# Output projection of a decoder step joined to the last attention head: partial products over seven heads, sample rows first

## The chip, the cores and the metric

One core of a Trainium2 chip runs one program that computes the whole step. Its engines are TensorE (PE, with its weight loads PEld), VectorE (DVE), ScalarE (ACT), GpSimd (POOL) and SyncE (SP), which here issues DMAs. Each runs its own list of instructions in order and meets the others only at semaphores. The metric is the device time of the program in microseconds; lower is better.

## The reference

One layer of a decoder trunk for 1024 prompt rows and 8 sample rows, all of width 1024 in float32:

```python
h = x * (1 + sc1) + sh1
q, k, v, u, gates = split(h @ w_in)                  # 8 heads, q1/q2/k1/k2 of 64, v of 128
o = attend(rope(q), rope(k), v, lam)                 # softmax(q1 k1) - lam * softmax(q2 k2)
attn_out = head_rmsnorm(o, subln_g) * (1 - lam_init)
merged = sigmoid(g_pool) * pool_mixer(u) + sigmoid(g_attn) * attn_out
x = layer_norm(alpha * x + (1 + g1) * (merged @ w_out), ln1_g, ln1_b)
h2 = x * (1 + sc2) + sh2
x = layer_norm(alpha * x + (1 + g2) * hier_moe(h2), ln2_g, ln2_b)   # 16 experts, 2 per row
```

The change concerns `merged @ w_out` and what lies on either side of it: the last head in front, the layer norm, `h2` and the routing of rows to experts behind.

## The kernel before

The program has five stages with a barrier on all five engines between them (`stage_end`: each adds one to a semaphore and waits for all). Stage 0 computes the modulation and `h`; stage 1 the pooling branch and the attention heads; stage 2 the output projection, layer norm, `h2`, router logits and routing; stage 3 the experts in 32 slots of 128 rows; stage 4 combines and normalises. Float32 products are made of three reduced-precision ones: each operand is split in a high part (ScalarE's copy) and a remainder (a subtraction on VectorE or GpSimd), and `mm3` (lines 856 to 860) runs high times remainder, remainder times high, high times high into one PSUM sum.

**Stage 1.** It begins with the sample state: SP loads it (line 632), TensorE transposes it (940 to 943) and waits until VectorE has copied it (1853) before the first projection piece. Then come twelve pieces of `u` with the pooling products. A piece is 24 matmuls of 344 columns (`piece`, 927 to 936). The heads loop (1120 to 1188) has eight steps for each head, one for each block of 128 rows. In a step TensorE makes the scores, ScalarE the exponentials (`exps`), VectorE maxima and the combination of the two softmaxes. `turn` transposes blocks of weights, `weights` on ScalarE and VectorE splits them, `product` multiplies them with v. There are ten turns for each head; four of them (6 to 9) run inside the next head, and for the last head behind the loop (1189 to 1191). Between these, TensorE runs pieces of the next head's input projection, as `filler`, to fill its waits; which ones is written in `step_pieces` (541 to 546). The last head has only its own six gate pieces left, in steps 4 to 7. A head ends with `squares` and `inverse_rms` (the RMS norm) and VectorE's `merge` (1983 to 1991), which adds the two branches; SP stores the merged rows of a head in DRAM (`merged_stored`, 684 to 686). The split `h` (`hT`) and the splits of `w_in` fill the SBUF tensor `R` up to the heads' own operands.

**Stage 2.** The split w_out takes the place of `hT`. SP loads w_out in eight parts of 512 KB and, from DRAM, each tile's merged columns for all eight heads (`tile3`, 733 to 740). ScalarE and VectorE split w_out, ScalarE and GpSimd (`m_rest`, 2335) the columns. `project` (1197 to 1209) makes 48 matmuls of 512 columns for one tile of 128 rows; nine tiles, the last with the 8 sample rows. Two pairs of PSUM banks take turns, and two buffers of columns. VectorE's `norm3` (2078 to 2088) does gate, residual and layer norm; GpSimd's `second_input` (2340 to 2347) makes `h2`; TensorE transposes it (`turn_rows3`), ScalarE copies it (`columns`), TensorE makes the logits (`router`), VectorE adds the bias (`logits`). For the sample tile the tables of the prompt are overwritten by those of the samples (771 to 773, 2103 to 2106). Then routing runs on VectorE (2125 to 2191) until the barrier.

## Time and profile before

| quantity | value |
|---|---|
| median of three runs | 1553.48 us (1551.81 to 1553.80) |
| profiled execution, its time | 1553.97 us |
| span of its instructions | 1552.1 us |
| TensorE busy, share of the span | 1315.6 us, 85% |
| VectorE busy | 988.1 us, 64% |
| ScalarE busy | 716.6 us, 46% |
| GpSimd busy | 284.5 us, 18% |
| TensorE on the chain that ended last | 67% |

All positions in the text are microseconds from the start of the span. A busy time is that of an engine's instructions; matmuls overlap a little, so the time that one costs is read from the distance of starts, not from its own duration. Idle time stands in brackets behind an instruction, with what ended it. The granted clock is TensorE's: 1.00 is 2.4 GHz, 0.50 is 1.2 GHz.

### The profile page before, as it was taken

The page shows a single profiled execution, that of the slowest core. Times are in us where ns is not written, and L with a number is a line of the kernel's source. Part 1 is how long each engine was busy: PE and PEld are TensorE (multiplying, and loading weights), DVE is VectorE, ACT ScalarE, POOL GpSimd, SP SyncE. Part 2 cuts the span into 40 slices and gives each one's busy share as a digit, 9 for nine tenths or more (in the row PEclk, how much of TensorE's full clock was granted, in tenths as well). Part 3 has the DMA queues.
Part 4 walks back from the last instruction along what each step waited for, and adds up shares of the span by engine and source line. Part 5 has one row for each costly group of instructions (what it writes and reads, how often), then busy time and mean ns, then how long its engine had stood idle before and what let it go on. Part 6 is the DMA issues. An engine that isn't in the chain of part 4 may idle for free.

```text
span 1552.1 us, 24627 instructions
## 1 busy us (share of the span) xinstructions
PE 1315.6 (85%) x8748; PEld 1139.0 (73%) x8748; DVE 988.1 (64%) x1484; ACT 716.6 (46%) x1249; POOL 284.5 (18%) x161
## 2 busy tenths in 40 slices
PE   6698989999999999999998783899549999999800
PEld 3488979898988989899897572677338887888600
DVE  2334357576674758657485633456459998999669
ACT  1344334444543535444454424011118897999612
POOL 1422111011111111111111001344231111111050
PEclk9899989999999999999999785899659999999955
DMA  9686433232233323233232106633139989556393
GB/s 313 199 267 207 128 87 91 80 90 77 83 96 87 105 71 94 75 84 102 85 97 65 49 7 222 189 109 123 45 106 328 319 298 370 184 202 222 124 294 141
DMA packets 211362, 229.53 MB, mean 148 GB/s; under 512 B 18070, under 2 KB 185178, under 8 KB 211131
## 3 DMA queue, kind: packets, MB, share of 16 engines
q1 hardware_dynamic: 196011, 173.52, 35.3%
q0 software_dynamic: 6976, 25.23, 5.0%
q10 hardware_dynamic: 8280, 29.51, 4.8%
q8 instruction: 59, 0.97, 0.3%
q14 instruction: 36, 0.29, 0.1%
HBM read 173.20 MB, written 46.79 MB: 142 GB/s over the span
## 4 chain that ended last, share of the span: by engine, by line
PE 67%; DVE 14%; ACT 5%; DMA 5%; issue 4%; SPq 3%; POOL 2%; ACTq 0%; DVEq 0%; POOLq 0%
PE S L858 6%; PE S L860 6%; PE S L859 6%; PE T L931 4%; PE T L932 4%; PE PB L931 4%; PE T L935 4%; PE PB L935 4%; PE PB L932 4%; PE S L1021 3%; ACT F L1345 3%; DVE F L1931 2%; PE T L1047 2%; PE T L1107 2%; DVE sm L1915 2%
## 5 line engine op out<-in xcount | busy, mean ns | idle before, releaser
L1345 ACT ACTIVATE R<-F 128x1024 fp32r<-128x1024 f32 (+3 forms) x302 | 292.6, 1014 | 125.0 <-DVE F L1806 46.0
L858 PE MATMUL S<-R 128*128 128x512 f32 (+1 forms) x528 | 213.2, 404 | 34.6 <-ACT R L1345 19.6
L859 PE MATMUL S<-R 128*128 128x512 f32 (+1 forms) x528 | 209.4, 397 | 0.0
L860 PE MATMUL S<-R 128*128 128x512 f32 (+1 forms) x528 | 209.3, 396 | 0.0
L2316 POOL TENSOR_TENSOR R<-F,R 128x1024 fp32r<-128x1024 f32 x40 | 99.7, 2494 | 593.5 <-ACT R L1345 593.5
L931 PE MATMUL T<-R 128*128 128x344 f32 x480 | 158.6, 335 | 0.0
L931 PE MATMUL PB<-R 128*128 128x344 f32 x480 | 157.6, 333 | 0.0
L932 PE MATMUL T<-R 128*128 128x344 f32 x480 | 153.0, 323 | 0.0
L932 PE MATMUL PB<-R 128*128 128x344 f32 x480 | 152.0, 321 | 0.0
L858 PEld LDWEIGHTS S<-R 128*128 128x128 f32 (+1 forms) x528 | 99.9, 189 | 61.4 <-issue 35.7
L1345 ACT ACTIVATE R<-T 128x512 fp32r<-128x512 f32 x144 | 82.7, 596 | 118.2 <-PE T L1047 76.0
L1345 ACT ACTIVATE F<-T 128x344 f32<-128x344 f32 (+5 forms) x100 | 42.1, 425 | 205.7 <-PE T L935 113.8
L1345 ACT ACTIVATE F<-S,sm 128x256 f32<-128x256 f32 (+7 forms) x128 | 93.6, 739 | 79.5 <-DVE sm L1915 42.4
L860 PEld LDWEIGHTS S<-R 128*128 128x128 f32 (+1 forms) x528 | 99.6, 189 | 23.4
L859 PEld LDWEIGHTS S<-R 128*128 128x128 f32 (+1 forms) x528 | 99.9, 189 | 21.3
L931 PEld LDWEIGHTS T<-R 128*128 128x128 f32 x480 | 91.5, 191 | 1.9 <-issue 1.8
L1912 DVE TENSOR_REDUCE sm<-S 128x1 f32<-128x128 f32 (+3 forms) x32 | 15.7, 491 | 120.3 <-PE S L1024 120.3
L2381 POOL DMA_INDIRECT F<-h_d,idxs x32 | 46.4, 1448 | 250.4 <-PE T L1267 230.6
L932 PEld LDWEIGHTS T<-R 128*128 128x128 f32 x480 | 91.7, 191 | 0.7 <-issue 0.7
L931 PEld LDWEIGHTS PB<-R 128*128 128x128 f32 x480 | 90.8, 189 | 1.7 <-issue 1.6
L932 PEld LDWEIGHTS PB<-R 128*128 128x128 f32 x480 | 90.9, 189 | 1.0 <-issue 1.0
L2199 DVE TENSOR_TENSOR R<-F,R 128x1024 fp32r<-128x1024 f32 x62 | 75.8, 1222 | 20.6 <-ACT R L1345 20.6
(258 smaller groups left out, 2747.5 us busy)
## 6 DMA issues: line engine op xcount, KB each, us to landing
F<-in_w_ada SPq DMA_DIRECT2D x24, 1024.0 KB
F<-in_w_in SPq DMA_DIRECT2D x44, 512.0 KB, 4.0
F<-in_w_e_gate SPq DMA_DIRECT2D x16, 1024.0 KB
F<-in_w_e_up SPq DMA_DIRECT2D x16, 1024.0 KB
F<-in_w_e_down SPq DMA_DIRECT2D x16, 1024.0 KB
y_d<-F ACTq DMA_DIRECT2D x32, 512.0 KB, 7.4
out<-F SPq DMA_DIRECT2D x24, 512.0 KB, 4.0
F<-F SPq DMA_DIRECT2D x192, 43.0 KB, 1.9
```

What stands on the lines that cost most here:

```text
L858: mm(out, w[0], m[1], start=start, stop=False)
L859: mm(out, w[1], m[0], start=False, stop=False)
L860: return mm(out, w[0], m[0], start=False, stop=stop)
L931: mm(bank[:, 0:PIECE], whl[b][0][:, k, :], x[1][:, k, :], start=(k == 0), stop=False)
L932: mm(bank[:, 0:PIECE], whl[b][0][:, k, :], x[0][:, k, :], start=False, stop=False)
L935: last = mm(bank[:, 0:PIECE], whl[b][1][:, k, :], x[0][:, k, :], start=False, stop=(k == KC - 1))
L1021: mm(S[:, m * SEQ + a:m * SEQ + a + n], qhl[x][half, i * P:(i + 1) * P], khl[y][half, a:a + n], start=(x == 0 and y == 1), stop=(x == 0 an ...
L1047: last = tr(TB[0][:, (2 * j + t) * P:(2 * j + t + 1) * P], block_rows(h, 2 * p + t)[:, (2 * g + j) * P:(2 * g + j + 1) * P], ident)
L1345: return nc.scalar.activation(out, in_, func, **kw)
L2199: TT(gu[b][1][:, k, 0:FF], raw_g[b][:, k, :], gu[b][0][:, k, 0:FF].bitcast(F32), ALU.subtract).then_inc(g_lo, 1)
L2316: nc.gpsimd.tensor_tensor(whl[c % 2][1], wraw2[c % 2], whl[c % 2][0].bitcast(F32), ALU.subtract).then_inc(w_lo.sem, 1)
L2381: nc.gpsimd.indirect_dma_start(out=xg[b], out_offset=None, in_=h2_d, in_offset=bass.IndirectOffsetOnAxis(ap=idxs[:, tile:tile + 1], axis=0 ...
```

## The change

- The barrier between heads and output projection is gone; four stages are left. Every engine goes on in its own list, with semaphores for each buffer.
- In the last head the six gate pieces run one in each of the steps 0 to 5. Their results go to the places of the head's q and k rows.
- When these pieces are done, `hT` is free, and the split w_out goes there. Its eight parts are loaded from step 1 of the last head on, into five buffers in place of the four in one block. ScalarE splits them in steps 5 to 7 and in the last turns, GpSimd makes all eight remainders.
- TensorE makes the products of the first three tiles over heads 0 to 6 inside the last head and behind it (`unit`), the product over head 7 after the merge, with columns split straight from SBUF (`last_hi`, `last_lo`). The sample rows are tile 0.
- Three PSUM pairs and three buffers of columns take turns, where there were two; the PSUM tensors are laid out anew. The first three tiles take heads 0 to 6 from DRAM, the other six all eight heads after the last store.
- Transposes and router products stand at written places between quarters of a tile, transposes in two halves through one bank; the loops are unrolled. All logits stay in one PSUM bank, and the bias is added once at the end.
- The layer norm's scale and shift goes from VectorE to ScalarE (`normal`); the additions of 1 to the first gate are part of VectorE's first instruction. VectorE makes `h2` of the last tile itself. The samples' tables have buffers of their own and come with the others; VectorE's last merge waits for all thirteen tables.
- In stage 1 the transposes of the sample state come behind the second piece, not ahead of the first.

The core of the diff:

```diff
-    TB = [ctx.enter_context(nc.psum_tensor(f"T{i}", [P, 512], F32)) for i in range(2)]
+    T0 = ctx.enter_context(nc.psum_tensor("T0", [P, 512], F32))
+    AB = ctx.enter_context(nc.psum_tensor("AB", [P, 1024], F32))
     OB = ctx.enter_context(nc.psum_tensor("OB", [P, 512], F32))
-    PB = ctx.enter_context(nc.psum_tensor("PB", [P, 512], F32))
+    TB = [T0, AB[:, 0:512]]
+    PB = AB[:, 512:1024]
...
-            return [first + j for j in {4: (0,), 5: (1,), 6: (2, 3), 7: (4, 5)}.get(i, ())]
+            return [first + i] if i < 6 else []
...
+            def w_out_chunk(k):
+                b = k % 5
+                if k >= 5:
+                    sp.wait_ge(wo_lo, k - 4)
+                    sp.wait_ge(wo_hi, k - 4)
+                sp.dma_start(wo32[b], wov[:, k, :]).then_inc(wo_landed[b].sem, 16)
+
+            def columns3(n):
+
+                b, (t, rows) = n % 3, at3(n)
+                heads = 7 if n < 3 else 8
+                if n >= 3:
+                    sp.wait_ge(mg_st, 16 * H)
+                    sp.wait_ge(m_hi, n - 2)
+                    sp.wait_ge(m_lo, n - 2)
+                sp.dma_start(mt32[b][:, 0:heads, 0:rows], mg_d.rearrange("k p n -> p k n")[:, 0:heads, t * P:t * P + rows]).then_inc(m_landed[b].sem, 16)
+
+            def rows3(n):
+
+                t, rows = at3(n)
+                if n >= 2:
+                    sp.wait_ge(var_done, n - 1)
+                sp.dma_start(x3[n % 2][0:rows, :], x_p[t * P:t * P + rows, :] if n else x_s).then_inc(x3_landed[n % 2], 16)
...
+            def first_w_out():
+                chunk_split(sp, N_CHUNKS - 2)
+                chunk_split(sp, N_CHUNKS - 1)
+                for k in range(3):
+                    w_out_chunk(k)
...
+                sp.wait_ge(kout_st, 16 * H)
+                w_out_chunk(3)
+                sp.wait_ge(vout_st, 16 * H)
+                v_lo.wait(sp, H - 1, 0)
+                w_out_chunk(4)
...
+            def last_tables():
+                for k in range(5, 8):
+                    w_out_chunk(k)
+                gate0_used.wait(sp, H - 1, 2)
+                table(l1b, I["ln1_b"].to_broadcast([P, D]))
+                os_ready.wait(sp, H - 1, 0)
+                table(g1s[0:NS, :], mod_d[1:9, 2 * D:3 * D])
+                table(sc2s[0:NS, :], mod_d[1:9, 4 * D:5 * D])
+                comb.wait(sp, H - 1, 7)
+                columns3(2)
+                rows3(0)
+                for k, dst, src in ((5, l1g, I["ln1_g"]), (6, sc2b, mod_d[0:1, 4 * D:5 * D]), (7, sh2b, mod_d[0:1, 3 * D:4 * D])):
+                    sp.wait_ge(wo_hi, k + 1)
+                    sp.wait_ge(wo_lo, k + 1)
+                    table(dst, src.to_broadcast([P, D]))
+                table(sh2s[0:NS, :], mod_d[1:9, 3 * D:4 * D])
+                t_ready.wait(sp, H - 1, 9)
+                rows3(1)
+
...
             merged_stored(H - 1)
+            columns3(3)
+            columns3(4)
+            columns3(5)
+            rows3(2)
+            columns3(6)
+            rows3(3)
+            columns3(7)
+            rows3(4)
+            columns3(8)
+            sp.wait_ge(h2_done, 1)
...
-        pe.wait_ge(ld_pool, 16)
-        for g in range(4):
-            last = tr(TB[0][:, 120 * g:120 * g + 120], stt[0:120, g * P:(g + 1) * P], ident[0:120, 0:120])
-        last.then_inc(stT_ready, 1)
-        pe.wait_ge(stT_copied, 1)
...
+                if n == 1:
+                    state_columns()
...
+        def unit(n, k, halves=(0, 1)):
+
+            rows = at3(n)[1]
+            if k == 0:
+                pe.wait_ge(m_hi, n + 1)
+                pe.wait_ge(m_lo, n + 1)
+                if n == 0:
+                    copied(pe, LAST + 4)
+                    copied(pe, LAST + 5)
+                else:
+                    exp_done.wait(pe, H - 1, 7)
+                if n == 2 and 0 in halves:
+                    ln_done.wait(pe, H - 1, 0)
+            if k == KC - 1:
+                mb_hi.wait(pe, n + 1)
+                mb_lo.wait(pe, n + 1)
+            if n == 0:
+                pe.wait_ge(wo_hi, k + 1)
+                pe.wait_ge(wo_lo, k + 1)
+            for q in halves:
+                last = mm3(WB[n][0:rows, 512 * q:512 * q + 512], [m[:, k, 0:rows] for m in mhl[n]],
+                           [w[:, k, 512 * q:512 * q + 512] for w in wo], start=(k == 0), stop=(k == KC - 1))
+            if k == KC - 1:
+                last.then_inc(wout_ready, 1)
...
+                if h == H - 1 and i >= 6:
+                    todo = [lambda k=k: unit(0, k) for k in ((0, 1), (2, 3))[i - 6]]
...
+            unit(*((0, 4), (0, 5), (0, 6), (1, 0))[n - 6])
             product(H - 1, n)
-        exp_done.wait(pe, H - 1, 7)
+        for k in range(1, 4):
+            unit(1, k)
         squares(H - 1)
-        stage_end(pe, 1)
-
-
-        def project(n, b, rows, first=False):
-            pe.wait_ge(m_hi, n + 1)
-            pe.wait_ge(m_lo, n + 1)
-            if not (isinstance(n, int) and n < 2):
-                pe.wait_ge(wout_used, n - 1)
-            for q in range(2):
-                for k in range(KC):
-                    if first and q == 0:
-                        pe.wait_ge(wo_hi, k + 1)
...
+        def project(n, q, ks):
+            b = n % 3
+            if q == 0 and ks[0] == 0:
+                pe.wait_ge(m_hi, n + 1)
+                pe.wait_ge(m_lo, n + 1)
+                pe.wait_ge(wout_used, n - 2)
+            for k in ks:
+                last = mm3(WB[b][:, 512 * q:512 * q + 512], [m[:, k, :] for m in mhl[b]],
+                           [w[:, k, 512 * q:512 * q + 512] for w in wo], start=(k == 0), stop=(k == KC - 1))
+            if q == 1 and ks[-1] == KC - 1:
+                last.then_inc(wout_ready, 1)
...
+        BETWEEN = {4: ((), (lambda: ta(0),), (), (lambda: tb(0),)),
+                   5: ((lambda: router(0), lambda: ta(1)), (lambda: tb(1),), (lambda: router(1),), ()),
+                   6: ((lambda: ta(2),), (lambda: tb(2),), (lambda: router(2), lambda: ta(3)), (lambda: tb(3),)),
+                   7: ((lambda: router(3), lambda: ta(4)), (lambda: tb(4),), (lambda: router(4),), (lambda: ta(5),)),
+                   8: ((lambda: tb(5),), (lambda: router(5), lambda: ta(6)), (lambda: tb(6),), (lambda: router(6),))}
+        for n in range(3, 9):
+            for e in range(4):
+                project(n, e // 2, range(4 * (e % 2), 4 * (e % 2) + 4))
+                for extra in BETWEEN.get(n, ((),) * 4)[e]:
...
+        def w_out_hi(k):
+            wo_landed[k % 5].wait(act, 16 * (k // 5 + 1))
+            if k == 0:
+                ready(act, LAST + 5)
+            act_(wo[0][:, k, :], wo32[k % 5]).then_inc(wo_hi, 1)
...
+                    if h == H - 1:
+                        w_out_hi(0)
+                        merged_hi(0)
...
+            if n < 9:
+                w_out_hi(n - 1)
         outputs(H - 1, 3)
         squares(H - 1)
+        merged_hi(2)
         inverse_rms(H - 1)
-        stage_end(act, 1)
...
+        def normal(n):
+            rows = at3(n)[1]
+            off3_done.wait(act, n + 1)
+            act_(y3[0:rows, :], y3[0:rows, :], ACT.Identity, scale=rstd1[0:rows, :], bias=off3[0:rows, :]).then_inc(norm3_done.sem, 1)
...
+            if h == H - 1:
+                tables3()
...
+        def last_lo(n):
+
+            t, rows = at3(n)
+            mb_hi.wait(dve, n + 1)
+            TT(mhl[n][1][:, 7, 0:rows], poolc[:, t * P:t * P + rows], mhl[n][0][:, 7, 0:rows].bitcast(F32), ALU.subtract).then_inc(mb_lo.sem, 1)
...
+        def sums3(n):
+
+            b, rows = n % 2, at3(n)[1]
+            y = y3[0:rows, :]
+            dve.wait_ge(wout_ready, n + 1)
+            mark(STT(out=y, in0=(g1b if n else g1s)[0:rows, :], scalar=1.0, in1=WB[n % 3][0:rows, :], op0=ALU.add, op1=ALU.mult), wout_used, n + 1)
+            dve.wait_ge(x3_landed[b], X3 + 16 * (n // 2 + 1))
+            V(STT(out=y, in0=x3[b][0:rows, :], scalar=ALPHA, in1=y, op0=ALU.mult, op1=ALU.add))
             for q in range(2):
-                V(nc.vector.bn_stats(stat[0:rows, q, :], y[0:rows, 512 * q:512 * q + 512]))
...
+        def last_input():
+
+            dve.wait_ge(h2_st[0], 16 * 4)
+            dve.wait_ge(h2T_ready, 14)
+            V(TT(h2t[0], x1t[0], sc2b, ALU.mult))
+            TT(h2t[0], h2t[0], sh2b, ALU.add).then_inc(h2_last.sem, 1)
+
+        for n in range(9):
+            sums3(n)
+            offset3(n)
+            affine3(n)
+        last_input()
...
+        def w_out_lo(k):
+            wo_landed[k % 5].wait(pool, 16 * (k // 5 + 1))
+            pool.wait_ge(wo_hi, k + 1)
+            nc.gpsimd.tensor_tensor(wo[1][:, k, :], wo32[k % 5], wo[0][:, k, :].bitcast(F32), ALU.subtract).then_inc(wo_lo, 1)
...
+        w_out_lo(0)
+        m_rest(0)
+        w_out_lo(1)
+        w_out_lo(2)
+        m_rest(1)
+        for k in range(3, KC):
+            w_out_lo(k)
+        m_rest(2)
+        m_rest(3)
+        m_rest(4)
+        pool.wait_ge(tab_landed, 16 * TABLES)
+        pool.wait_ge(tab_ready, 1)
+        pool.wait_ge(mg_st, 16 * H)
+        for n in range(8):
+            second_input(n)
+            if n < 4:
+                m_rest(n + 5)
+        pool.wait_ge(h2T_ready, 18)
```

## Rows read from the trace of the kernel before

**Rows 1.** Busy time by stretch: PE, PEld, DVE, ACT, POOL, clock, DMA, GB/s.
```profile
180.00:930.00 750.00, 709.10 (x4813) 645.11 (x4813) 471.97 (x800) 328.74 (x671) 92.36 (x37) 0.97 0.28 81
930.00:1151.00 221.00, 145.68 (x686) 116.10 (x684) 115.68 (x179) 44.03 (x61) 72.91 (x32) 0.77 0.36 121
```
**Rows 2.** Chain that ended last, projection stage: start, duration, what.
```profile
933.84 1.62 issue
...
938.09 1.16 PE T L1083 x2
...
944.89 2.65 DMA mg_d<-F
...
997.03 0.43 PE S L858
...
1051.65 1.69 PE PB L1223 x16
...
1065.47 1.70 PE PB L1223 x16
...
1105.71 3.57 PE PB L1223 x16
```
**Rows 3.** Timeline of TensorE: start, duration, instruction, idle time before and what ended it.
```profile
958.82 0.76 PE L858 MATMUL S<-R 128*128 128x512 f32 x1 [19.59 <-ACT R L1345]
...
995.41 0.77 PE L858 MATMUL S<-R 128*128 128x512 f32 x1 [7.42 <-POOL R L2337]
```
**Rows 4.** Timeline of VectorE, last full tile and routing.
```profile
1079.47 1.22 DVE L2081 TENSOR_TENSOR F<-S,F 128x1024 f32<-128x1024 f32 x1 [3.91 <-PE S L860]
...
1086.51 1.22 DVE L2088 TENSOR_TENSOR F<-F 128x1024 f32<-128x1024 f32 x1
...
1118.45 0.19 DVE L1791 TENSOR_REDUCE F<-F 128x9 f32<-128x36 f32 x1
...
1150.42 0.17 DVE L2191 TENSOR_SCALAR te<-F 1x32 int32<-1x32 f32 x1
```
**Rows 5.** Timeline of TensorE, two matmuls of the projection, 41 apart.
```profile
978.31 0.39 PE L858 MATMUL S<-R 128*128 128x512 f32 x1
...
987.61 0.39 PE L860 MATMUL S<-R 128*128 128x512 f32 x1
```
**Rows 6.** Chain that ended last, start of the pooling stage.
```profile
67.41 2.92 DMA F<-in_state_pool
...
72.33 0.65 PE S L931
```
**Rows 7.** Timeline of TensorE in head 7, with the waits before.
```profile
860.79 2.63 PE L1083 MATMUL S<-F,cst 128*128 128x344 f32 x4 [3.62 <-DVE R L1935]
...
871.62 2.18 PE L1021 MATMUL S<-R 64*128 64x512 f32 x12 [4.49 <-ACT F L1345]
...
905.11 0.41 PE L931 MATMUL PB<-R 128*128 128x344 f32 x1
...
908.98 0.28 PE L858 MATMUL OB<-R 128*128 128x256 f32 x1
...
920.58 0.45 PE L858 MATMUL OB<-R 128*128 128x256 f32 x1 [1.50 <-DVE R L1935]
```
**Rows 8.** Timeline of ScalarE: a split of w_out, a normalisation of the last stage.
```profile
951.51 1.06 ACT L1345 ACTIVATE R<-F 128x1024 fp32r<-128x1024 f32 x1 [9.31 <-DMA F<-in_w_out]
...
1502.28 1.24 ACT L1345 ACTIVATE F<-F 128x1024 f32<-128x1024 f32 x1
```
**Rows 9.** GpSimd and VectorE side by side, and VectorE's line in the stage (min/median/max, ns).
```profile
992.82 2.33 POOL L2337 TENSOR_TENSOR R<-F,R 128x1024 fp32r<-128x1024 f32 x1
...
993.11 2.60 DVE L2075 TENSOR_SCALAR F<-F,sm 128x1024 f32<-128x1024 f32 x1
...
L2075 DVE TENSOR_SCALAR F<-F,sm x9: 801/814/2597, 983.8 to 1102.1; 128x1024 f32<-128x1024 f32 x8, 8x1024 f32<-8x1024 f32 x1
```
**Rows 10.** Loads of merged columns by SP (line 737), issue to landing.
```profile
DMA to landing us min/median/max: 5.5/7.0/9.8
```

More of the change, by code:

```diff
@@ new lines, in turn_rows3 @@
+        def turn_rows3(n, c, bank):
+            rows = at3(n)[1]
+            if c == 0:
+                if n < 8:
+                    pe.wait_ge(h2_done, n + 1)
+                else:
+                    h2_last.wait(pe, 1)
+            if bank is T0:
+                pe.wait_ge(h2T_copied, 2 * n + c)
+            for k in range(4 * c, 4 * c + 4):
+                last = tr(bank[:, (k % 4) * P:(k % 4) * P + rows], h2t[n % 2][0:rows, k * P:(k + 1) * P], ident[0:rows, 0:rows])
+            last.then_inc(h2T_ready, 1)
@@ L1427, in take @@
             if n == 12 and h:
-                merged.wait(act, h - 1, 0)
+                if h < H - 1:
+                    merged.wait(act, h - 1, 0)
+                else:
+                    kt_ready.wait(act, h, 4)
             ready(act, g)
@@ new lines, in _ @@
+        ca, cb = (lambda n: columns(n, 0, T0)), (lambda n: columns(n, 1, T0))
+        tile3(3)
+        tile3(4)
+        deviation(0)
+        normal(0)
+        deviation(1)
+        x1_store(0)
+        normal(1)
+        tile3(5)
+        deviation(2)
+        x1_store(1)
+        normal(2)
+        h2_store(0)
+        ca(0)
+        x1_store(2)
+        h2_store(1)
+        tile3(6)
+        cb(0)
+        deviation(3)
+        normal(3)
+        ca(1)
+        cb(1)
+        x1_store(3)
@@ new lines, in _ @@
+        h2_store(2)
+        tile3(7)
+        deviation(4)
+        normal(4)
+        ca(2)
+        x1_store(4)
+        cb(2)
+        h2_store(3)
+        tile3(8)
+        deviation(5)
+        normal(5)
+        ca(3)
+        x1_store(5)
+        cb(3)
+        h2_store(4)
+        ca(4)
+        deviation(6)
+        normal(6)
+        cb(4)
+        x1_store(6)
+        h2_store(5)
+        ca(5)
+        cb(5)
+        deviation(7)
+        normal(7)
+        ca(6)
+        x1_store(7)
@@ L1681, in _ @@
+        h2_store(6)
+        cb(6)
+        ca(7)
+        h2_store(7)
+        cb(7)
+        deviation(8)
+        normal(8)
+        h2_store(8)
+        columns(8, 0, T0)
+        columns(8, 1, Sb[0])
+        x1_store(8)
         act.wait_ge(route_exp, 1)
@@ L2336, in m_rest, with second_input @@
             pool.wait_ge(m_hi, n + 1)
-            nc.gpsimd.tensor_tensor(mhl[b][1][:, :, 0:rows], mt32[b][:, :, 0:rows], mhl[b][0][:, :, 0:rows].bitcast(F32), ALU.subtract)\
+            nc.gpsimd.tensor_tensor(mhl[b][1][:, 0:heads, 0:rows], mt32[b][:, 0:heads, 0:rows], mhl[b][0][:, 0:heads, 0:rows].bitcast(F32), ALU.subtract)\
                 .then_inc(m_lo, 1)
-        def second_input(n, b, rows, before):
+        def second_input(n):
+            b, rows = n % 2, at3(n)[1]
+            scale, shift = (sc2b, sh2b) if n else (sc2s, sh2s)
@@ L2352, in _ @@
[L2352 to L2364 removed]
+            if n >= 2:
+                pool.wait_ge(h2_st[b], 16 * (n // 2))
+                pool.wait_ge(h2T_ready, 2 * n - 2)
```

417 lines of the change are left out of this document (186 added, 231 removed).

## Prediction

> **What bounds the kernel now.** I read the views in this order: the page's slices, busy time by stage, the waits and the timeline of TensorE around the end of the heads, the chain, and last the timelines of VectorE, ScalarE and GpSimd in the same place. In the heads TensorE is the bound: 709 of 750 us busy at a mean granted clock of 0.97 [rows 1]. In the 221 us from the end of the heads to the start of the experts it is busy for 146 us at a mean clock of 0.77 [rows 1]. So this stage has 75 us in which TensorE does nothing, and it is here that a reordering can pay. The stretch has three holes. First: the last product of head 7 ends at 933.84, six sums of squares run from 935.46 to 939.25 [rows 2], and the next matmul, the first of the output projection, starts at 958.82 after 19.6 us of idle time [rows 3]. The chain through that hole is the merge (done at 944.87), the store of the merged rows (2.65 us, lands 947.5) [rows 2], barrier, load of w_out, split. Second: the third tile waits 7.4 us for GpSimd [rows 3], whose remainder for it was queued behind the first tile's h2. Third: the eight sample rows come last and cost as much on every engine as a full tile. VectorE takes the last full tile at 1079.47, and routing begins at 1118.45, 39 us later [rows 4]. Routing itself runs to 1150.6 and I expect none of its 32.1 us to change.
>
> Between the holes the projection is bound by TensorE. At full clock 41 matmuls of 512 columns lie between 978.31 and 987.61, 0.227 us each; at half clock the chain has 0.43 each [rows 2, 5]. One unit (one contraction block, both halves of the output, three split products each) is six matmuls, 1.36 us. A tile is eight units, 10.9 us. From router to router in the loop it is 1065.47 - 1051.65 = 13.8 us [rows 2], so one router and one set of transposes cost 2.9 us between two tiles.
>
> **Part 1, the state transposes at the start of the pooling stage.** SP issues the state load at 67.41, right behind the barrier; TensorE waits for it, transposes, waits for VectorE's copy and starts its first real product at 72.33 [rows 6]. The change lets the first product start at about 67.4 and puts the four transposes two pieces later. They take at most the time from landing (70.33) to 72.33 less VectorE's copy, about 1.2 us. Gain 4.9 - 1.2 = 3.7 us at most; zero at worst, if the modulation weights, which are loaded in the same stretch and are needed 5 us earlier, are late. I take 3. TensorE bounds the stages behind, so it should last.
>
> **Part 2, inside head 7.** Six gate pieces of 3.87 us (905.11 to 908.98) [rows 7] were run at steps 4 to 7 as 1, 1, 2, 2; now one runs at each of steps 0 to 5. In steps 0 and 1 each falls into a wait for VectorE like that of 1.50 us at 920.58 [rows 7], so each adds some 2.4. In step 2 it lies in the 3.62 us wait, in step 3 in the 4.49 us wait [rows 7], which cost nothing more; and the array stays at full clock, worth about 1.4. Step 4 thus starts 3.5 us late. In steps 6 and 7 four pieces (15.5 us) make room for four units of the sample rows (5.5). Of these 10 us I count only 2.8, because what is late next is not TensorE: VectorE has its maxima and combinations in these steps anyway, and each unit waits for its eighth of w_out, which is ScalarE 1.06 [rows 8] and then GpSimd 2.3 to 2.4 [rows 9] after a ScalarE instruction that itself waits for the exponentials. Those splits are queued on ScalarE ahead of the head's own weights and outputs; the products stand behind the units on TensorE. So the first of the last four turns starts 0.7 late. These turns went round in 3.9 us each: turn, ScalarE, VectorE, then the product after a 1.5 us wait at half clock. A unit fills the wait; but ScalarE 0.6 + 1.06 and GpSimd 2.4 lie between a turn and the second unit behind it, so I get 12.3 us instead of 15.4 with the first wait for a remainder. The last product ends at 933.8 + 0.7 + 0.5 - 3.1 = 931.9. Bounds: 8 us earlier (the 10 us come in full), 8 us later (each of the eight remainders costs a microsecond).
>
> **Part 3, from the last product to the fourth tile.** TensorE has three units (4.1), the squares (3.8 in the trace [rows 2], after a wait; with none I take 2.5, between that and half of it), ten units (13.6) and the three last blocks (4.1): 24.3 us, to 956.2. Meanwhile the merge: squares end at 931.9 + 6.6 = 938.5; before it took from 939.25 to 944.87, 5.6 us, so it ends at 944.1. VectorE now also waits inside the merge for thirteen tables, the last issued behind the last w_out remainder. That is about 931, with a landing of up to 9.8 like the loads of [rows 10]: 941, and the reciprocal roots it waits for anyway come at 941.6. Free, but with under 1 us in hand. The three last-head splits follow in 1.5 us, ahead of 956. So the merge is covered by products. Not covered is the way of the next tile: store 2.65, load median 7.0 (5.5 to 9.8) [rows 2, 10], ScalarE 1.06, GpSimd 2.4, hand-overs 0.6, in all 13.7: ready at 957.8. TensorE waits 1.6 us and then runs some nine matmuls at half clock (0.2 more each, 1.8): it goes on at 959.6. Bounds: no wait (956.2), or 9.8 for the load and a 4 us store (962).
>
> The barrier and the w_out load behind it are gone, and so is the third tile's wait for GpSimd, since its columns are split ahead of any h2. Three pairs let VectorE fall behind by three tiles. It needs 8.3 us a tile (1079.47 to 1087.73) [rows 4] plus 0.8 for the hand-over to ScalarE and up to 1 for GpSimd in the way. It starts at 954 and meets TensorE's 13.8 us rhythm at the sixth tile or so, before any product must wait for its pair.
>
> **Part 4, the loop.** Six tiles, each with a router and transposes: 6 x 13.8 = 82.9, one more set of transposes 0.9, and 1 for places where a copy of transposed columns stands on ScalarE behind a tile that VectorE still has. Last projection done at 1044.4; with part 1 at 1041.4. Before: 1079.5.
>
> **Part 5, the tail.** The last tile is now a full one, the sample rows went first, their tables came early, and the load before 1097 is gone. VectorE: 8.3 for the tile less 0.81 plus ScalarE's normalisation (1.24 for the same form in the last stage [rows 8]) plus 0.4 for a small instruction and hand-overs: 9.1. Then h2 on VectorE, two instructions, 2.5, in place of GpSimd's 4.8. Router 3.57 at half clock [rows 2], the eight transposes 1.8 (in the loop the 2.9 less the router's 1.7 is 1.2; twice 0.9 is the matmuls alone), copy 0.7, logits 0.6. Sum 18.3, where it was 39. Routing starts at 1059.7 instead of 1118.45: 58.7 us earlier, and everything behind keeps its length; the first experts' weights still come before it. The chip's profiled execution of before took 1553.97 (0.5 over the median of the three runs), so the sum is 1553.97 - 58.7 = 1495.3, and 1494.8 against the median: **1495**.
>
> **A rule that speaks against it.** At 993.11 VectorE's scale-and-shift takes 2.60 us, while GpSimd's subtraction started at 992.82 and ends at 995.15; the median of the line is 0.81 [rows 9]. So a GpSimd instruction can hold a VectorE one until it is through. The change gives GpSimd the eight w_out remainders, which VectorE computed before in a stretch with nothing else to do.
> The Trainium skill (SBUF — State Buffer, Who interferes with whom) says that the two share a port pair as an exclusive lock, that VectorE's 2-port modes and its instructions with two SBUF inputs contend with GpSimd's reads, and that the first to start blocks the other fully. By that rule every combination of head 7 may be held; the trace agrees at 993, but the line's median stayed at 0.81 beside a busy GpSimd. What it would do to the time is the second rival below.
>
> **The rivals.**
> 1. *The load takes the barrier's place.* The fourth tile's columns wait for the store, then for one of three loads issued together. For it: landings of up to 9.8 us; against it: 24 us of products stand before. At the bounds above plus a second late tile: 6 us more, 1501.
> 2. *GpSimd becomes the bound of head 7.* Eight remainders, each blocking a VectorE instruction for up to 2.60 - 0.81 = 1.8 us, 14 us in all: 1509. For it: rows 9, and the products queue behind the units. Against it: the median of that line, 0.81, with GpSimd busy in the same stretch.
> 3. *More than I count.* Steps 6 and 7 give TensorE's 10 us in full, no wait at the fourth tile: 10 us less, 1485.
> 4. *The overlap doesn't come about.* Units find no split w_out and hold up the head; the projection's first 21 units (28.6 us) then lie after the products as before: about 1524.
> 5. *Slower than before.* The projection runs at half clock from end to end: 432 matmuls at 0.20 us more are 86 us, 1581. It decides from 59 us lost, that is if over two thirds of the 432 run at half clock. Against it: before, full clock was back at 978.31 after the 19.6 us hole [rows 3, 5], and the changed order has fewer holes.
>
> **How the numbers follow.** Forecast 0.60 (1487 to 1503), rival 1 0.13, rival 2 0.10, rival 3 0.11, rival 4 0.04, rival 5 0.02. The range for 8 in 10 takes the forecast with rivals 1, most of 2 and most of 3: 1483 to 1511. A measurement can tell 0.2% (3 us) from no change. Only rival 5 is slower; faster 0.97, same 0.01, slower 0.02.
>
> **What would show it.** Right: no idle time over 3 us on TensorE between the last turns and the last projection; the last product of head 7 within 8 us of 931 (928 with part 1); the last projection near 1041; 18 us from there to the first routing maximum; 32 us of routing. Part 1: the first product of the pooling stage near 67.4. Wrong: idle time at the fourth tile over 4 us (rival 1); VectorE's combinations in head 7 at 2 us or more, or units waiting for GpSimd (rival 2); a clock of 0.5 inside the loop (rival 5).

## The result, and the profile after

The changed kernel takes 1506.55 us (median of 4 runs, 1503.01 to 1508.82) where the kernel before took 1553.62: a ratio of 0.9697, 95% interval 0.9685 to 0.9709. The forecast was 1495 with a range of 1483 to 1511. So the range held the time, and the point was 11.5 us too low. The profiled execution of the changed kernel took 1508.82 us, with a span of 1506.6.

First the page: TensorE's busy time and granted clock by slices, and the chain by engine. Up to the end of the projection (the first 28 slices) the clock now never falls below 8 tenths; the 5 and the 6 are the tail and the routing.

```profile
PE 1307.6 (87%) x8748; PEld 1132.1 (75%) x8748; DVE 995.8 (66%) x1472; ACT 726.3 (48%) x1261; POOL 308.4 (20%) x167
PEclk9989989999999999999999999999569999999955
PE 68%; DVE 16%; ACT 5%; issue 4%; DMA 4%; SPq 2%; POOL 1%; ACTq 0%; DVEq 0%; POOLq 0%
```

Busy time by stretch (PE, PEld, DVE, ACT, POOL, clock, DMA, GB/s): the end of head 7 with the first units, the projection from there on, and the tail up to the routing.

```profile
930.00:958.00 28.00, 26.97 (x130) 20.89 (x129) 8.89 (x11) 10.33 (x15) 6.83 (x3) 1.00 0.48 145
958.00:1057.00 99.00, 90.10 (x455) 74.03 (x454) 71.31 (x72) 26.83 (x37) 57.22 (x22) 0.95 0.42 145
1057.00:1075.00 18.00, 12.03 (x65) 10.95 (x63) 9.47 (x12) 5.21 (x7) 0.00 (x0) 0.61 0.22 87
```

The hole of 19.6 us in [rows 3] is gone: TensorE is busy for 27 of 28 us there. In the loop it is busy for 90 of 99 us; of those 9 us the forecast had 1.6, at the fourth tile, and 1 for late copies. TensorE's timeline with its waits: the start of the pooling stage (three rows), head 7 (two), the fourth tile, and one of the loop.

```profile
62.50 1.08 PE L965 MATMUL S<-F 128*9 128x64 f32 x64 [1.25 <-DMA F<-in_b_ada]
...
69.77 0.66 PE L982 MATMUL S<-R 128*128 128x344 f32 x1 [3.75 <-DVEq L249]
...
78.94 1.90 PE L965 MATMUL S<-F 128*9 128x64 f32 x64 [3.05 <-DMA F<-in_b_ada]
...
900.25 0.48 PE L909 MATMUL AB<-R 128*8 128x512 f32 x1 [2.88 <-POOL R L2545]
...
907.49 0.59 PE L909 MATMUL AB<-R 128*8 128x512 f32 x1 [2.99 <-POOL R L2539]
...
963.06 0.47 PE L909 MATMUL AB<-R 128*128 128x512 f32 x1 [2.24 <-POOL R L2545]
...
999.74 1.12 PE L1315 MATMUL T<-cst,F 128*128 128x128 f32 x4 [2.48 <-ACT F L1443]
```

VectorE in the projection. The first tile, the offset of 8x1 elements (L2283) and two instructions of 1024 columns are long; then come the last two tiles, which wait for TensorE again, and the first maximum of the routing.

```profile
958.14 1.21 DVE L2271 SCALAR_TENSOR_TENSOR F<-F,AB 8x1024 f32<-8x1024 f32 x1 [8.49 <-PE AB L911]
...
963.07 2.10 DVE L2283 SCALAR_TENSOR_TENSOR sm<-sm 8x1 f32<-8x1 f32 x1 [0.23 <-DVE sm L2282]
...
970.24 2.35 DVE L2273 SCALAR_TENSOR_TENSOR F<-F 128x1024 f32<-128x1024 f32 x1
...
982.27 2.28 DVE L2273 SCALAR_TENSOR_TENSOR F<-F 128x1024 f32<-128x1024 f32 x1
...
1042.64 1.22 DVE L2271 SCALAR_TENSOR_TENSOR F<-F,S 128x1024 f32<-128x1024 f32 x1 [5.98 <-PE S L911]
...
1057.16 1.22 DVE L2271 SCALAR_TENSOR_TENSOR F<-F,S 128x1024 f32<-128x1024 f32 x1 [5.75 <-PE S L911]
...
1075.36 0.19 DVE L1982 TENSOR_REDUCE F<-F 128x9 f32<-128x36 f32 x1
```

GpSimd and ScalarE beside them. The first row is GpSimd's remainders of the fourth and fifth tile's columns, one behind the other until 965.16. GpSimd's second instruction of h2 takes 3.23 us beside a busy VectorE, and ScalarE's split of the fourth tile's columns waits for TensorE, not for the load.

```profile
959.40 5.76 POOL L2545 TENSOR_TENSOR R<-F,R 128x1024 fp32r<-128x1024 f32 x2 [17.23 <-ACT R L1443]
...
969.12 2.39 POOL L2556 TENSOR_TENSOR F<-F 8x1024 f32<-8x1024 f32 x1 [3.96 <-DVE F L2294]
...
983.55 3.23 POOL L2557 TENSOR_TENSOR F<-F 128x1024 f32<-128x1024 f32 x1
...
958.20 1.06 ACT L1443 ACTIVATE R<-F 128x1024 fp32r<-128x1024 f32 x1 [8.88 <-PE AB L911]
```

The row at 970.24 can be read off against GpSimd's. VectorE's instruction starts 1.1 us after GpSimd's at 969.12, which ends at 971.51; 1.08 us after that, VectorE's is done (1.22 is its usual length). The offset at 963.07 is the same: 0.16 us of work, through (965.17) only when GpSimd's remainder is.

### The profile page after: what moved, and what is told of

Its sections match the earlier page's. It is cut to its first block, busy times and chain, and to the rows that moved or that the text cites. A ratio compares the mean times of both kernels' runs of the same rounds, so it can differ in the third digit from the quotient of the medians.

```text
span 1506.6 us, 24502 instructions
## 1 busy us (share of the span) xinstructions
PE 1307.6 (87%) x8748; PEld 1132.1 (75%) x8748; DVE 995.8 (66%) x1472; ACT 726.3 (48%) x1261; POOL 308.4 (20%) x167
## 4 chain that ended last, share of the span: by engine, by line
PE 68%; DVE 16%; ACT 5%; issue 4%; DMA 4%; SPq 2%; POOL 1%; ACTq 0%; DVEq 0%; POOLq 0%
PE AB L982 8%; PE AB L983 8%; PE AB L986 8%; PE S L909 6%; PE S L911 6%; PE S L910 6%; ACT F L1443 4%; PE S L1078 3%; DVE sm L2106 2%; DVE F L2122 2%; PE T L1166 2%; PE T L1104 2%; PE OB L909 1%; PE S L924 1%; ACT R L1443 1%
## 5 line engine op out<-in xcount | busy, mean ns | idle before, releaser
L1443 ACT ACTIVATE R<-F 128x1024 fp32r<-128x1024 f32 (+4 forms) x305 | 292.7, 1006 | 100.1 <-DVE F L1997 48.0
L982 PE MATMUL AB<-R 128*128 128x344 f32 x960 | 315.7, 333 | 0.0
L983 PE MATMUL AB<-R 128*128 128x344 f32 x960 | 304.6, 321 | 0.0
L909 PE MATMUL S<-R 128*128 128x512 f32 x480 | 193.9, 404 | 1.8 <-ACT F L1443 1.6
L911 PE MATMUL S<-R 128*128 128x512 f32 x480 | 189.1, 394 | 0.0
L910 PE MATMUL S<-R 128*128 128x512 f32 x480 | 188.9, 394 | 0.0
L982 PEld LDWEIGHTS AB<-R 128*128 128x128 f32 x960 | 181.7, 189 | 3.4 <-issue 3.2
L983 PEld LDWEIGHTS AB<-R 128*128 128x128 f32 x960 | 182.0, 190 | 1.7 <-issue 1.7
L986 PE MATMUL AB<-R 128*128 128x344 f32 x960 | 171.6, 320 | 0.0
L1443 ACT ACTIVATE F<-AB 128x344 f32<-128x344 f32 (+1 forms) x126 | 56.1, 447 | 221.7 <-PE AB L986 221.0
L986 PEld LDWEIGHTS AB<-R 128*128 128x128 f32 x960 | 155.7, 188 | 0.0
L1443 ACT ACTIVATE R<-T 128x512 fp32r<-128x512 f32 x112 | 66.9, 597 | 113.2 <-PE T L1104 71.3
L909 PEld LDWEIGHTS S<-R 128*128 128x128 f32 x480 | 91.6, 191 | 21.2 <-issue 2.9
L911 PEld LDWEIGHTS S<-R 128*128 128x128 f32 x480 | 91.3, 190 | 20.1
L910 PEld LDWEIGHTS S<-R 128*128 128x128 f32 x480 | 91.4, 191 | 17.9
L2593 POOL DMA_INDIRECT F<-h_d,idxs x32 | 50.4, 1576 | 244.2 <-PE AB L1365 227.2
L2126 DVE TENSOR_TENSOR R<-T,R 128x512 fp32r<-128x512 f32 x80 | 54.7, 684 | 45.0 <-ACT R L1443 45.0
L1443 ACT ACTIVATE F<-S 9x64 f32<-9x64 f32 (+3 forms) x159 | 53.6, 349 | 50.8 <-PE S L986 29.6
```

The lines of the kernel that those rows point to most:

```text
L909: mm(out, w[0], m[1], start=start, stop=False)
L910: mm(out, w[1], m[0], start=False, stop=False)
L911: return mm(out, w[0], m[0], start=False, stop=stop)
L982: mm(bank[:, 0:PIECE], whl[b][0][:, k, :], x[1][:, k, :], start=(k == 0), stop=False)
L983: mm(bank[:, 0:PIECE], whl[b][0][:, k, :], x[0][:, k, :], start=False, stop=False)
L986: last = mm(bank[:, 0:PIECE], whl[b][1][:, k, :], x[0][:, k, :], start=False, stop=(k == KC - 1))
```

## The experiments

Positions in a profile shift by some us with the early stages. So each kernel is read by four marks: Z, the second modulation piece of stage 0 (62.50 above); X, head 6's scores at 797.40 in the changed kernel (793.78 in the one before); E, the end of head 7's last product; L, VectorE's first instruction of the last tile. T is the first product of the fourth tile.

| kernel | Z to X | X to E | E to T | T to L | median us | ratio to before |
|---|---|---|---|---|---|---|
| before | 733.7 | 140.1 | | | 1553.5 | 1 |
| changed | 734.9 | 139.7 | 26.0 | 94.1 | 1506.6 | 0.9697 |
| c1 changed again | 735.0 | 140.0 | 26.0 | 94.1 | 1505.8 | 0.9685 [0.9661, 0.9710] |
| e1 state first | 733.2 | 138.3 | 25.9 | 92.1 | 1504.7 | 0.9689 [0.9673, 0.9705] |
| e2 tile 0 early | 733.4 | 139.8 | 23.6 | 92.7 | 1501.6 | 0.9675 [0.9651, 0.9699] |
| e3 rows in PSUM | 734.1 | 139.9 | 30.9 | 83.9 | 1502.4 | 0.9671 [0.9652, 0.9691] |
| e4 units behind | 732.7 | 140.7 | 38.4 | 94.2 | 1517.8 | 0.9765 [0.9750, 0.9780] |
| e6 e2 with e3 | 733.6 | 138.3 | E to L 111.6 | | 1497.4 | 0.9639 [0.9626, 0.9653] |
| e7 h2 halved | 733.7 | 138.2 | 25.9 | 90.7 | 1502.8 | one run |
| e8 e1, e2, e3 | 733.2 | 138.4 | E to L 111.6 | | 1496.0 | 0.9626 [0.9613, 0.9639] |
| e9 thin remainders | 733.9 | 133.3 | 25.9 | 94.0 | 1499.0 | one run |
| e10 e8, ScalarE's order | 733.0 | 139.8 | E to L 107.8 | | 1494.3 | 0.9618 [0.9604, 0.9631] |

From L to the routing's first maximum it is 18.2 to 18.4 us in each of them, and from there to the end of the span 430.4 to 434.1. The intervals of e1, e2 and e3 overlap that of c1, so for these three the marks carry the argument and not the time; e4, e6, e8 and e10 lie clear of it.

**c1, the changed kernel again.**

> The changed kernel itself, as the control for the three beside it on the same chip. Expected 1503 to 1509 us, as measured so far; the place of the last projection's end, of the first routing maximum and of the first scores of head 7 are read from it.

1505.84 us, and every mark behind Z within 0.3 us of the first profile. The kernel repeats; what moves is Z (2.7 us earlier here).

**e1, the state's transposes back where they were** (part 1 undone).

```diff
+        state_columns()
+        pe.wait_ge(stT_copied, 1)
...
-                if n == 1:
-                    state_columns()
```

> The changed kernel with the transposes of the sample state back ahead of the first piece, as before. My theory: the earlier start is eaten by the modulation weights that come late (TensorE waited 3.05 us for them at 78.94 and then ran a piece at half clock), so this kernel is 0 to 2 us faster than the control. The prediction's own term: it is 3 us slower than the control.

The first product of the pooling stage starts late again, as in [rows 6]:

```profile
72.38 0.66 PE L982 MATMUL S<-R 128*128 128x344 f32 x1 [0.82 <-DVE F L2043]
```

but the wait for the modulation weights behind the first pieces (3.05 us at 78.94 above) shrinks to 0.54, and Z to X is 1.7 us shorter than in the changed kernel. Over all profiles, Z to X is 732.7 to 735.0 with the transposes moved (mean 733.9 of eight) and 733.0 to 733.7 with them first (mean 733.3 of four). 1504.67 against 1505.84 is no difference that these runs can tell. The move gains nothing: the pieces start 4.9 us earlier (67.53 in c1) and wait for the modulation's weights.

**e2, tile 0's last block early:** the last head's unit of the sample rows runs before the second half of tile 2, not behind all ten units.

```diff
+        unit(0, 7)
         for k in range(7):
             unit(2, k, (0,))
-        for n in range(3):
+        for n in range(1, 3):
```

> The changed kernel with one unit moved: the last block of tile 0 (the sample rows) runs between the two halves of tile 2, not behind them. Theory A (the wait at the fourth tile is for tile 0's column buffer, and VectorE's queue of tiles bounds what follows): VectorE starts tile 0 about 5 us earlier, the 2.2 us wait of TensorE at the fourth tile shrinks to under 1, and the kernel is 2 to 5 us faster than the control. Rival B (the store and load of the merged columns bound the fourth tile, and TensorE bounds the rest): the wait stays and the time stays within 1 us.

The 2.24 us at the fourth tile are gone, since tile 0's column buffer comes free before the next split needs it:

```profile
957.54 0.39 PE L909 MATMUL AB<-R 128*128 128x512 f32 x1
...
959.21 0.15 DVE L2283 RECIPROCAL sm<-sm 8x1 f32<-8x1 f32 x1 [4.83 <-ACT sm L1444]
```

E to L falls by 3.9 us (120.1 to 116.2). VectorE starts tile 0 4.8 us earlier behind E, but then waits 4.83 us for ScalarE's root: the root is queued behind two splits, and the second of them waits for TensorE. So theory A holds by the marks and rival B does not; the time, 1501.6 against 1505.8, is not resolved.

**e3, the rows being normalised stay in their PSUM pair.** Three of VectorE's instructions of 1024 columns in each tile then read one operand from PSUM and one from SBUF instead of two from SBUF (the first one read the pair before, and the statistics have one input); GpSimd's work is the same. ScalarE's normalisation works in the pair too. The pair comes free with x1 instead of with the first instruction.

```diff
-            y = y3[0:rows, :]
+            y = WB[n % 3][0:rows, :]
...
+            dve.sem_inc(wout_used, 1)
```

> The changed kernel with the layer norm's row kept in its PSUM pair through all steps, so that no large VectorE instruction of the norm has two inputs in SBUF; the same instructions otherwise, and each pair is held until the tile is done. Theory A (GpSimd holds VectorE's instructions, 2.3 us of each tile's 11.5, and that backlog costs 9 us by the last projection): no large instruction of the norm over 1.4 us, a tile in 9.5 us or less, last projection 5 to 9 us earlier, time 1498 to 1502. Rival B (the place of the transposes and copies in the lists bounds, not VectorE's speed): tiles in 9.5 us, but the last projection within 1.5 us of the control. Rival C (a pair held longer makes TensorE wait for it): 3 us or more slower than the control.

VectorE's timeline in e3, and GpSimd's beside it, then the fourth tile:

```profile
974.47 1.23 DVE L2273 SCALAR_TENSOR_TENSOR S<-F,S 128x1024 f32<-128x1024 f32 x1
...
974.03 2.41 POOL L2558 TENSOR_TENSOR F<-F 128x1024 f32<-128x1024 f32 x1
...
1012.26 2.10 DVE L2283 SCALAR_TENSOR_TENSOR sm<-sm 128x1 f32<-128x1 f32 x1
...
964.37 0.77 PE L909 MATMUL AB<-R 128*128 128x512 f32 x1 [7.16 <-DVEq L2296]
```

Started 0.44 us behind GpSimd's, the same line that took 2.35 us now takes its 1.23, and GpSimd's takes 2.41. No instruction of 1024 columns in the loop is over 1.23 us; only the offset, whose operands all lie in SBUF, is still held. T to L is 83.9 us, 10.2 less than in the changed kernel. TensorE is busy through all of it, and nine of its matmuls run at half clock. The gain is half eaten at the fourth tile, which waits 7.16 us for tile 0's pair: E to L falls by 5.3 us only. T thus comes 4.9 us later, which lets VectorE catch up, so e3 alone leaves open how much of the 10.2 is that; e10 below, with T at 23.6 us behind E, needs 84.3 for the same stretch. Theory A holds for the instructions, but not for every tile: most take 8.9 to 9.8 us, two take 12.9 and 13.3, with waits of 2.8 and 2.9 us for ScalarE's root. Rival B does not hold. Rival C's wait for a pair is there, at one place, but the kernel is not slower.

**e4, no units inside head 7:** the eight of steps 6 and 7 and of the four turns run behind its last product.

```diff
-                if h == H - 1 and i >= 6:
-                    todo = [lambda k=k: unit(0, k) for k in ((0, 1), (2, 3))[i - 6]]
...
-            unit(*((0, 4), (0, 5), (0, 6), (1, 0))[n - 6])
```

> The changed kernel with the eight units of steps 6 and 7 and of the four turns of head 7 taken out of the head and put behind its last product; all else as changed. This prices the filling alone. Theory (the units fill waits of TensorE, at the price of 3 us waits for GpSimd's remainders at two of them): the last product of head 7 comes 3 to 6 us earlier than in the changed kernel, eight units more (10.9 us) then stand behind it, and the loop that follows is as before, so the last tile's sums come 3 to 8 us later and the time is 1509 to 1514. Rival (the units in the head gain nothing, since each wait for a remainder costs what it fills): last product 10 to 11 us earlier, the same time as the changed kernel, 1506.

```profile
903.02 0.58 PE L909 MATMUL OB<-R 128*128 128x256 f32 x1 [5.20 <-DVE R L2125]
...
932.03 0.58 PE L909 MATMUL OB<-R 128*128 128x256 f32 x1 [1.41 <-DVE R L2125]
```

Both theories miss. The last product comes 0.7 us later than with the units, not 3 to 11 earlier, and E to T grows by 12.4. The whole is 12.0 us slower. So the eight units in the head cost nothing at all: without them TensorE waits for VectorE instead, and no matmul there waits for GpSimd.

**e9, thin remainders.** What is left out: GpSimd takes 64 of 1024 columns of each remainder of w_out.

> The changed kernel, but GpSimd takes only the first 64 of 1024 columns of each of the eight remainders of w_out (the other columns of the remainder keep what the memory held, so the rows behind are other numbers; only the marks up to the routing are read). It takes away about 18 us of GpSimd's work in and before head 7. Theory (GpSimd's remainders hold VectorE there and TensorE waits for both): VectorE's two combinations of 3.1 and 3.3 us take 1.15 and 1.28 as before the change, the combination with the gate 0.5 instead of 2.1, TensorE's waits for GpSimd in head 7 (3.2, 2.7, 1.0, 1.0, 0.5, 0.4) go to under 1 in all, the last product of head 7 ends 5 to 8 us nearer to the first scores of head 6 (140.0 in the changed kernel) and everything behind follows. Rival (the head is paced by ScalarE's and VectorE's own chain, and the held instructions lie beside it): the instructions shorten but the last product comes at most 2 us earlier.

GpSimd's first long one in head 7 and VectorE's combination, first in the changed kernel (904.85 and 905.17), then the combination of e9:

```profile
904.85 5.67 POOL L2539 TENSOR_TENSOR R<-F,R 128x1024 fp32r<-128x1024 f32 x2 [4.70 <-ACT R L1443]
...
905.17 3.12 DVE L2122 SCALAR_TENSOR_TENSOR F<-F,sm 128x896 f32<-128x896 f32 x1
```

```profile
901.13 1.15 DVE L2122 SCALAR_TENSOR_TENSOR F<-F,sm 128x896 f32<-128x896 f32 x1
...
912.89 1.28 DVE L2122 SCALAR_TENSOR_TENSOR F<-F,sm 128x1024 f32<-128x1024 f32 x1
```

X to E falls by 6.7 us, and the time of the one run by as much (1498.97). Against the shorter of head 7's two lengths (last section) it is 5.0. One part of the theory misses: the first unit still waits 2.79 us for GpSimd, for a remainder of merged columns that itself waits for ScalarE. Head 7 is thus paced by the chain of ScalarE, VectorE and GpSimd; GpSimd's eight remainders cost it 5.0 to 6.7 us, and the units themselves nothing. In e4 the combinations are held as before (3.13 and 3.29 us) and the head stays long though TensorE waits for no remainder. That speaks for VectorE's holds as the way the price is paid; but TensorE's granted clock at the end of the head is also lower in e4 (0.70 from 892.8 to 933.6, against 0.91 in c1 from 894.8 to 934.9), and no run separates the two.

**e7, GpSimd's multiplication left out.** h2 is then x1 plus the shift.

> The changed kernel, but GpSimd leaves out the multiplication of h2 by its scale for tiles 0 to 7 (h2 is then x1 plus the shift; the experts' inputs and the routing are other numbers, so only the marks up to the routing are read). Theory (an instruction of GpSimd with both inputs in SBUF and one of VectorE exclude each other): half as many of VectorE's instructions in the loop are held at 2 us or more (13 in the changed kernel's seven first tiles), none of the held ones where GpSimd is idle, VectorE's period falls from 11.8 to 10.5 us or less, and the last tile's sums come 4 to 9 us nearer to the last product of head 7 (120.1 us in the changed kernel). Rival (VectorE's long instructions come from something else, PSUM or the DMA traffic): as many long ones, and 120 us.

Nine of VectorE's instructions in the loop are over 2 us, where c1 has eleven (the expectation's 13 was a miscount). E to L is 116.6, 3.5 less: below the bound given, and the count is not halved; a tile takes VectorE 11.0 us (11.5 in c1), not 10.5. Leaving out half of h2 takes away fewer meetings than e3 makes harmless, since the remainders and the other half of h2 still meet VectorE. By itself e7 would not carry the cause; e3 does.

**e6, e2 and e3 together,** with tile 0's row left in SBUF so that its pair comes free at once, and **e8,** the same with e1.

> Tile 0's last block runs early (as in e2), and the rows being normalised stay in their PSUM pair for tiles 1 to 8 (as in e3), while tile 0's row still leaves its pair with the first VectorE instruction. In e3 no product of the loop waited any more, but the fourth tile waited 7.2 us for tile 0's pair, because the pair was held until x1 was through. Theory (GpSimd holds VectorE's instructions that have both inputs in SBUF; the pair of tile 0 costs e3 its gain): no VectorE instruction of 1024 columns over 1.4 us, no wait at the fourth tile, from its first product to the last tile's sums 84 to 85 us (94.1 in the changed kernel, 83.9 in e3), from the last product of head 7 to there 107 to 109 us (120.1 in the changed kernel); 11 to 12 us less than the changed kernel, about 1494. Rival (the two gains of e2 and e3 are of the same wait and don't add): 1500. Rival (ScalarE's order bounds the loop): VectorE waits for ScalarE's root in more tiles than e3's three, and 1498 or more.

> As e6, and the state's transposes stand before the first product of the pooling stage again (part 1 undone, as in e1). Theory (moving them gains nothing, because TensorE then waits for the modulation weights instead): within 2 us of e6 on either side, rather faster by 1, and from the end of stage 0 to head 7 the 733.2 us of e1 and not the 735.0 of the changed kernel. Rival (moving them is worth its 3 us and e1's profile was chance): 3 us slower than e6.

E to L is 111.6 in both, 2.6 us over the theory's bound. The medians, 1497.4 and 1496.0, lie between the theory and the first rival and beside the second one's 1498: VectorE waits for ScalarE's root in four tiles, e3's three and tile 0 (4.83 us), so ScalarE's order has a share. e8 against e6 (1.4 us, Z to X 733.2) is as the theory said: moving the transposes gains nothing. No wait at the fourth tile, but one at the fifth; e6, and VectorE in e8:

```profile
971.28 0.47 PE L909 MATMUL S<-R 128*128 128x512 f32 x1 [4.22 <-DVEq L2300]
```

```profile
957.53 0.15 DVE L2284 RECIPROCAL sm<-sm 8x1 f32<-8x1 f32 x1 [4.82 <-ACT sm L1443]
```

**e10, ScalarE takes tile 0's root before the fifth tile's split.**

```diff
         tile3(3)
-        tile3(4)
         deviation(0)
         normal(0)
+        tile3(4)
```

> As e8, with one line moved: ScalarE takes tile 0's root and normalisation before it splits the fifth tile's columns. In e8 VectorE waited 4.8 us for that root, because the split ahead of it waited until TensorE was through with tile 1's columns, and so the fifth tile's first product waited 4.2 us for tile 1's pair. Theory (that hole is ScalarE's order and nothing else): VectorE's wait falls to about 1.9 us (a table load and the root), the 4.2 us at the fifth tile go to under 1, from the last product of head 7 to the last tile's sums 107.5 us (111.5 in e8), and the time is 1492, 4 us less than e8. Rival (the pairs are then late at the next tiles, which only moves the wait): the same wait at the sixth or seventh tile and 1496 again.

```profile
954.81 0.15 DVE L2284 RECIPROCAL sm<-sm 8x1 f32<-8x1 f32 x1 [0.60 <-ACT sm L1443]
...
958.21 3.30 DVE L2297 TENSOR_TENSOR F<-F 8x1024 f32<-8x1024 f32 x1
...
970.51 0.47 PE L909 MATMUL S<-R 128*128 128x512 f32 x1 [2.10 <-DVEq L2299]
```

E to L is 107.8. VectorE's wait went from 4.82 to 0.60; the wait at the fifth tile only halved, because tile 0's last instruction, with both operands in SBUF as all of tile 0's are here, now meets GpSimd. T to L is 84.3, with these 2.10 us in it. 1494.3 us: 0.9618 of the kernel before, 11.5 us less than c1, and the lowest median of all. Against e8 it gains 1.7 us in the medians, with intervals that overlap, and not the 3.8 of its marks; its profiled head 7 was 1.4 us longer (last section).

## Why the prediction was right or wrong

The sum was made for a profiled execution: 1495.3. The profile of the changed kernel has 1508.82. By the marks, the difference of 13.5 us is made of these (they add up to 13.3; the rest lies outside the span). The forecast's fourth tile starts at 957.8; its 1.8 us of half clock behind that stand in T to L:

| step | forecast | measured | difference |
|---|---|---|---|
| stage 0 (Z) | 60.1 | 62.5 | +2.4 |
| part 1: Z to X | 730.7 | 734.9 | +4.2 |
| part 2: X to E | 138.1 | 139.7 | +1.6 |
| part 3: E to T | 25.9 | 26.0 | +0.1 |
| part 4: T to L | 86.6 | 94.1 | +7.5 |
| part 5: L to routing | 18.3 | 18.2 | -0.1 |
| routing to the end | 433.6 | 431.2 | -2.4 |

**Part 1** was wrong. The step that failed is "I take 3", between 3.7 and zero: its own lower bound named what happened, that the modulation weights loaded in the same stretch come late. TensorE waited 3.05 us for them, and e1 and e8 show that undoing the move costs nothing. That is 3.0 of the 4.2 us; the other 1.2 lie within the 2.3 us over which Z to X varies.

**Part 2** came within 1.6 us by luck. I counted 1.9 us of gain in all and had no term for VectorE's instructions held by GpSimd. Without the long remainders (e9) X to E is 133.3, 6.8 us less than before the change. So the room was over three times what I counted, and GpSimd's remainders took nearly all of it. Squares were cheaper than said, 1.5 us and not 2.5.

**Part 3** had the right time for a wrong reason. Forecast: the fourth tile waits 1.6 us, ready through store and load, and goes on behind nine matmuls at half clock. Measured: 2.24 us, and no half clock behind it (0.39 us each from the second matmul on). But the load was not what came last. In e8 SP issues it at 946.56 and ScalarE's split starts at 950.49, 3.9 us later and not the 7.0 of [rows 10]. What held it was the column buffer of tile 0, free only at 957.9 since its last unit stood behind ten others. e2 shows it by moving that unit. The forecast didn't follow the three column buffers, only the three PSUM pairs.

**Part 4** was the large miss, 7.5 of 13.5 us, and the failed step is one term of VectorE's tile: "up to 1 for GpSimd in the way". It measured 2.7. From tile to tile it is 11.5 us (seven starts from 955.85 to 1024.63 in c1), and 8.8 without the holds, so the 8.3 and 0.8 beside the term were large enough. Eleven instructions of over 2 us, and a shorter one, meet GpSimd and are held for about 17 us in all: most of them 0.9 to 2.1 us each, the offset among them with 0.16 us of work. VectorE met TensorE's rhythm at the eighth tile (1042.64) and not at the sixth, and until then ScalarE's copies of transposed columns, queued behind it, let TensorE wait 2.77, 2.48 and twice 0.7 us (999.74 above is one of them): 6.7 us, with matmuls below full clock behind the waits (0.95 in the loop). With the meetings made harmless TensorE needs 82.1 us in e3 (83.9 less nine times 0.2 at half clock) and 82.2 in e10 (84.3 less its wait), so TensorE's own sum of 84.8 was 2.6 too long, and that hid part of the miss: the changed kernel loses 11.9 us in the loop.

**Part 5** was right to 0.1 us, and routing took 32.1 as forecast. From routing to the end the other changed kernels need 430.4 to 434.1 us, so the 2.4 us less lie within what this stretch varies by; no run tells why.

**The rule and the rivals.** The row at 993.11 in [rows 9] had shown the mechanism, and I set it aside for the line's median of 0.81. But the median passes over the few that meet, and says nothing of how many will meet in another order. In the kernel before VectorE had idle time between tiles, like the 3.91 us of [rows 4], and GpSimd's h2 mostly fell into it: three of VectorE's instructions from the third tile on were over 2 us. In the changed order VectorE works off a backlog for seven tiles without a gap, and eleven of its instructions are held over 2 us while GpSimd runs eighteen (959 to 1033). The second rival was the right mechanism, with the larger part of it at another place: it was to decide head 7 at 14 us and give 1509, nearer to the 1506.6 than the forecast. Head 7 paid 5.0 to 6.7 us; in the loop e3 got back 10.2 and e10 9.8. The first rival (the load) didn't come: e2 removed the wait without touching a load. The third had its room but not its gain. The fourth and fifth didn't come; the clock in the loop was 0.95.
The Trainium skill (SBUF — State Buffer, Who interferes with whom) states that VectorE's instructions with two SBUF inputs and GpSimd's that read SBUF exclude each other for the whole of an instruction, and that those with at most one SBUF input outside the 2-port modes don't contend. Both halves agree with the runs: 2.35 us with two and 1.23 us with one beside a busy GpSimd, and GpSimd's own 3.23 against 2.41.

## What to carry to other kernels

Before work goes to GpSimd, go through what VectorE will run beside it by its operands and by whether it still has gaps, not by a line's median: each instruction with two SBUF operands that meets one of GpSimd's may wait it out, however small it is, and a scale-and-shift with one may too (2.60 us in [rows 9]). For those with two, one operand left in PSUM took the wait away here. Follow every buffer of a rotation, not only the newest one, and each in-order queue behind it: twice here a small thing at its end (a last unit, a root behind a split) held what looked like a load or a pair. Filling an engine's waits is free only as long as what feeds the filling is.

## What the runs showed of the hardware that was not expected

- An instruction of 8x1 or 128x1 elements that takes 0.16 us alone took 2.1 to 2.3 us when it met GpSimd.
- Head 7 has two lengths, X to E 138.2 to 138.4 us in four profiles (e1, e6, e7, e8) and 139.7 to 140.0 in five (changed, c1, e2, e3, e10). In the first group, the units behind TensorE's second wait for GpSimd ran at full clock (0.40 us), in the second at half (0.59, as at 907.49 above). The waits before the first unit were 2.2 us in the first group and 2.9 to 3.3 in the second. That is 1.5 us of the spread from one kernel to another. One meeting goes with it in all nine. In the five long ones GpSimd's first remainder starts 0.15 to 0.17 us ahead of a VectorE instruction of 16x257 elements, which then takes 2.33 us or more; in the four short ones it starts 0.6 to 0.9 us behind that instruction's start, which takes 0.34. What moves the two by this much is open. The changed kernel first, then e8:

```profile
896.79 2.35 POOL L2539 TENSOR_TENSOR R<-F,R 128x1024 fp32r<-128x1024 f32 x1 [50.26 <-ACT R L1443]
...
896.94 2.34 DVE L2155 TENSOR_SCALAR F<-F,sm 16x257 f32<-16x257 f32 x1
```

```profile
893.90 0.34 DVE L2156 TENSOR_SCALAR F<-F,sm 16x257 f32<-16x257 f32 x1
```

- A load behind its store was there 3.9 us after its issue (e8, part 3 above), where the same loads in the loop of the kernel before had a median of 7.0 [rows 10].
